# The seven-product steps of a feed-forward kernel made twice as wide: two weight slots per step, 512 columns per product

## The chip, the cores and the metric

The kernel runs on one core of one Trainium2 chip. The metric is the device time of one execution in microseconds (us).

## The reference

One macaron layer over 256 tokens of width 2048, all in float32: half a SwiGLU feed-forward, a mixer (gated short convolution beside a sparse attention), another half feed-forward, and a final RMSNorm.

```
def swiglu(h, wg, wu, wd):
    return (jax.nn.silu(h @ wg) * (h @ wu)) @ wd
...
        x = x + 0.5 * swiglu(rmsnorm(x, ffn1_norm[i]), ffn1_wg[i], ffn1_wu[i], ffn1_wd[i])
        x = x + hybrid_mixer(rmsnorm(x, mix_norm[i]), w_in[i], conv_w[i],
...
        x = x + 0.5 * swiglu(rmsnorm(x, ffn2_norm[i]), ffn2_wg[i], ffn2_wu[i], ffn2_wd[i])
    return rmsnorm(x, final_norm)
```

D_MODEL is 2048 and D_FF 5632. The change touches the two feed-forwards alone.

## The kernel before, in words

**Slots.** Every weight is read once, in slots of 256 rows by 512 columns (two k-tiles of 128 rows; 512 KB). There are four slot buffers (`SLOTS`), and slot c lives in buffer c % 4. SP loads it into `raw`. ACT rounds it to `w_hi` (`hi`, L1236), DVE takes the remainder `w_lo = raw - w_hi` (`lo`, L1726), and TensorE multiplies the 256 tokens (two tiles of 128) by it (`group`, L739 to L741). Each float32 product is made of three matmuls: hi by hi, hi by lo, lo by hi. So a plain slot is 2 k-tiles x 2 token tiles x 3 = 12 matmuls of 512 columns.

**What waits for what.** `hi` of slot c waits for its landing and until TensorE has finished slot c - 4 (`group_done`). `lo` waits for `hi`, and its semaphore `lo_ready` lets TensorE start the slot and lets SP load slot c + 4. Each engine works through its own list in program order: whatever DVE has listed ahead of the `lo` of a slot holds TensorE up if it ends late.

**Seven-product slots.** In 115 of the 528 feed-forward slots the 2 x 2 blocks (two token tiles, two k-tiles, two column halves of 256) are multiplied with seven products in place of eight (the Strassen-Winograd scheme): `seven_products`, L764 to L766, is 21 matmuls of 256 columns. DVE makes four sums of weight blocks (`weight_sums`, L1793, L1796, L1798; buffer `wt`, two of them), ACT and DVE split them (`wt_hi` L1291, `wt_lo` L1806). Some products go straight into the result's banks, the others collect in PSUM banks 6 and 7. After the last seven-product slot of a job ACT copies one bank (`products_copy`, L1300), DVE combines them in `z` (`products_sum`, L1837 to L1842) and adds the result to the bank (`add_to_bank`, L1852) or to `x` (`add_to_x`, L1861).

**Order.** Per feed-forward: 11 chunks of 512 hidden columns, each 8 gate slots (banks 0 and 1) and then 8 up slots (banks 2 and 3). Chunks 1 to 10 hold three seven-product slots each, at places 6, 12 and 14 (`SEVEN_AT`). After chunks 0 to 5 comes the first down part (`down(0)`), after chunks 6 to 10 the second (`down(1)`): four column chunks of the output, 12 and 10 slots each, of which four and three are seven-product slots (in one column chunk two). The finished column chunk is added to `x` by `residual` (L1919). In the last column chunk of the program the last four slots are run for token tile 0 first and then for tile 1 (`tail`). The order of the slots is a list written out by hand (`down_order`), and DVE's and ACT's other steps are hung behind the slot of a given number. POOL moves the SwiGLU output's blocks by DMA (`gu_blocks`, L681), and ACT and DVE split it for the down part (`gu_operand`, L1325, L1899).

## Time and profile before

| | |
|---|---|
| median of 3 runs | 1846.38 us (1846.32 to 1847.37) |
| the profiled execution, its own time | 1847.15 us |
| its span, first to last instruction | 1845.3 us |
| granted TensorE clock, mean | 0.999 |
| busy share PE / DVE / ACT / POOL | 99% / 80% / 55% / 13% |
| DMA | 60.2% of the 16 engines' span, 199 GB/s |

PE is TensorE's matmuls, PEld its weight loads (they overlap), DVE VectorE, ACT ScalarE, POOL GpSimd, SP the queue that issues the loads. Matmuls are pipelined: one is listed with 0.39 us and the next begins 0.23 us after it, so a stretch is costed by the distance from start to start. "Releaser" is what ended an engine's wait.

### The profile page before, as it was taken

Reading aid. Unit: us, or ns where it says so; the run is one execution under the profiler, and the core shown is the slowest. Engines: PE = TensorE matmul, PEld = TensorE weight load, DVE = VectorE, ACT = ScalarE, POOL = GpSimd, SP = SyncE. Lnnn points to the kernel's source line nnn. Section 1 sums busy time; section 2 is a strip of 40 time slices with the busy share of each in tenths; the row PEclk is TensorE's granted clock in tenths of the full one; section 3 lists DMA queues with packets and bytes.
Section 4 is the critical chain, followed back from the end, with each engine's and each line's share of the span. In section 5 each row is a group of like instructions: output and inputs, shape, how many; then the busy total and the mean of one; then the engine's idle time right before and its main releaser. Section 6 shows DMA issues by size and latency. Waiting matters only on the chain.

```text
span 1845.3 us, 26275 instructions
## 1 busy us (share of the span) xinstructions
PE 1835.3 (99%) x9415; PEld 1560.1 (85%) x9415; DVE 1477.2 (80%) x1971; ACT 1007.5 (55%) x1309; POOL 244.8 (13%) x442
## 2 busy tenths in 40 slices
PE   9999999999999999999999999999999999999998
PEld 7888888888888888888788888888888888888887
DVE  6788889877888887678677866688889887888897
ACT  7555555444555565556567746454555545555554
POOL 1111111001111100000132200111111000221100
PEclk9999999999999999999999999999999999999999
DMA  7666666566666666766443655666676666666664
GB/s 262 195 207 215 207 203 212 196 203 209 206 205 205 200 200 203 217 209 198 142 140 100 217 183 193 207 195 206 203 221 201 205 199 193 211 215 209 217 195 158
DMA packets 199280, 367.19 MB, mean 199 GB/s; under 512 B 19012, under 2 KB 23856, under 8 KB 199056
## 3 DMA queue, kind: packets, MB, share of 16 engines
q1 hardware_dynamic: 185008, 352.37, 60.2%
q0 software_dynamic: 11648, 12.02, 2.2%
q10 hardware_dynamic: 2528, 1.52, 0.3%
q8 instruction: 61, 1.00, 0.2%
q14 instruction: 35, 0.29, 0.1%
HBM read 350.11 MB, written 4.19 MB: 192 GB/s over the span
## 4 chain that ended last, share of the span: by engine, by line
PE 96%; DVE 1%; ACT 1%; DMA 0%; issue 0%; POOL 0%; ACTq 0%; POOLq 0%; DVEq 0%
PE ps L739 26%; PE ps L740 26%; PE ps L741 26%; PE ps L766 5%; PE ps L765 5%; PE ps L764 5%; PE ps L797 2%; DVE w_lo L1726 1%; POOL gu_raw L681 0%; PE ps L1003 0%; PE ps L1030 0%; PE ps L1005 0%; PE ps L1031 0%; DMA gu_raw<-gu_sq 0%; PE ps L1133 0%
## 5 line engine op out<-in xcount | busy, mean ns | idle before, releaser
L1726 DVE TENSOR_TENSOR w_lo<-raw,w_hi 128x1024 fp32r<-128x1024 f32 x540 | 656.6, 1227 | 190.0 <-ACT w_hi L1236 187.8
L1236 ACT ACTIVATE w_hi<-raw 128x1024 fp32r<-128x1024 f32 x540 | 566.3, 1057 | 341.2 <-PE ps L741 299.0
L739 PE MATMUL ps<-w_hi,hT_hi 128*128 128x512 f32 x1516 | 593.7, 392 | 0.1
L740 PE MATMUL ps<-w_lo,hT_hi 128*128 128x512 f32 x1516 | 590.9, 390 | 0.0
L741 PE MATMUL ps<-w_hi,hT_lo 128*128 128x512 f32 x1516 | 590.4, 389 | 0.0
L741 PEld LDWEIGHTS ps<-w_hi,hT_lo 128*128 128x128 f32 x1516 | 284.6, 188 | 60.5
L681 POOL DMA_DIRECT2D gu_raw<-gu_sq x352 | 187.1, 540 | 1110.5 <-DVE gu_sq L1910 1033.0
L739 PEld LDWEIGHTS ps<-w_hi,hT_hi 128*128 128x128 f32 x1516 | 285.0, 188 | 57.1 <-DVE w_lo L1726 0.8
L740 PEld LDWEIGHTS ps<-w_lo,hT_hi 128*128 128x128 f32 x1516 | 285.0, 188 | 55.3
L1291 ACT ACTIVATE wt_hi<-wt 128x1024 fp32r<-128x1024 f32 x115 | 122.0, 1061 | 154.5 <-DVE wt L1798 154.5
L739 PE MATMUL ps<-w_hi,guT_hi 128*128 128x512 f32 x484 | 189.5, 391 | 1.0 <-DVE w_lo L1726 0.7
L740 PE MATMUL ps<-w_lo,guT_hi 128*128 128x512 f32 x484 | 189.0, 391 | 0.0
L741 PE MATMUL ps<-w_hi,guT_lo 128*128 128x512 f32 x484 | 188.3, 389 | 0.0
L1806 DVE TENSOR_TENSOR wt_lo<-wt,wt_hi 128x1024 fp32r<-128x1024 f32 x115 | 140.7, 1223 | 21.5 <-ACT wt_hi L1291 21.5
L1289 ACT ACTIVATE w_hi<-raw 128x768 fp32r<-128x768 f32 x115 | 97.3, 846 | 109.9 <-PE ps L741 92.1
L1804 DVE TENSOR_TENSOR w_lo<-raw,w_hi 128x768 fp32r<-128x768 f32 x115 | 109.3, 951 | 1.5 <-ACT w_hi L1289 1.5
L739 PEld LDWEIGHTS ps<-w_hi,guT_hi 128*128 128x128 f32 x484 | 91.1, 188 | 19.4 <-DVE w_lo L1726 1.4
L741 PEld LDWEIGHTS ps<-w_hi,guT_lo 128*128 128x128 f32 x484 | 90.9, 188 | 19.4
L740 PEld LDWEIGHTS ps<-w_lo,guT_hi 128*128 128x128 f32 x484 | 91.1, 188 | 16.8
L1793 DVE TENSOR_TENSOR wt<-raw 128x512 f32<-128x512 f32 x115 | 78.5, 683 | 0.0
L1300 ACT ACTIVATE z<-ps 128x512 f32<-128x512 f32 x56 | 33.5, 598 | 76.1 <-PE ps L766 76.1
L703 POOL TENSOR_SCALAR prob<-prob,sums,gate 128x128 f32<-128x128 f32 (+1 forms) x64 | 37.1, 589 | 257.5 <-DVE sums L2169 257.5
(298 smaller groups left out, 2423.3 us busy)
## 6 DMA issues: line engine op xcount, KB each, us to landing
raw<-in_ffn_wu_dram SPq DMA_DIRECT2D x176, 512.0 KB, 4.4
raw<-in_ffn_wd_dram SPq DMA_DIRECT2D x176, 512.0 KB, 4.5
raw<-in_ffn_wg_dram SPq DMA_DIRECT2D x175, 512.0 KB, 3.6
raw<-in_w_in_dram SPq DMA_DIRECT2D x88, 512.0 KB, 3.6
raw<-in_w_out_dram SPq DMA_DIRECT2D x32, 512.0 KB, 4.7
gu_raw<-gu_sq POOLq DMA_DIRECT2D x352, 32.0 KB, 3.6
x_parked<-x SPq DMA_DIRECT2D x8, 256.0 KB, 5.1
raw<-in_cmp_k_w_dram SPq DMA_DIRECT2D x8, 256.0 KB, 2.9
```

What stands on the lines that cost most here:

```text
L681: pool.dma_start(gu_raw[c_ * SQ:c_ * SQ + SQ, :, a_, :], gu_sq[a_ * SQ:a_ * SQ + SQ, :, c_ * P:c_ * P + P]).then_inc(gu_moved, 16)
L739: mm(o, x_hi, w_hi[:, s, kk, :], start=first and kk == 0, stop=False)
L740: mm(o, x_hi, w_lo[:, s, kk, :], start=False, stop=False)
L741: ins = mm(o, x_lo, w_hi[:, s, kk, :], start=False, stop=last and kk == GK - 1)
L764: mm(o, x_hi, y_hi[:, blk], start=opens, stop=False, skip_group_check=True)
L765: mm(o, x_hi, y_lo[:, blk], start=False, stop=False, skip_group_check=True)
L1236: act.activation(w_hi[:, c % SLOTS, :, :], raw[:, c % SLOTS, :, :], ACT.Copy).then_inc(hi_ready, 1)
L1289: act.activation(flat(w_hi, s)[:, HC:], flat(raw, s)[:, HC:], ACT.Copy).then_inc(hi_ready, 1)
L1291: act.activation(wt_hi[:, b, :], wt[:, b, :], ACT.Copy).then_inc(t_hi_ready, 1)
L1726: tt(w_lo[:, s, :, :], raw[:, s, :, :], w_hi[:, s, :, :].bitcast(F32), ALU.subtract).then_inc(lo_ready, 1)
L1804: tt(flat(w_lo, s)[:, HC:], flat(raw, s)[:, HC:], flat(w_hi, s)[:, HC:].bitcast(F32), ALU.subtract)
L1806: tt(wt_lo[:, b, :], wt[:, b, :], wt_hi[:, b, :].bitcast(F32), ALU.subtract).then_inc(lo_ready, 1)
```

## The change

A seven-product step now covers two slots that follow one another: the same two k-tiles of the gate and of the up chunk (`PAIR`, `PAIR2`), or of two down column chunks. The two column halves of the 2 x 2 scheme are these two chunks, so every product has 512 columns: 21 matmuls of 512 columns for two slots. There are 68 such pairs in place of 115 single slots: two in each of the 20 chunks, and 4 and 3 in each of the two halves of a down part.

- **Order.** In a chunk the gate slots of k 0 to 4 come first, a pair, gate 5, up 0 and 1, a pair, up 2 to 5. A down part is two halves (`h`); each half works on two column chunks at once, left in banks 0 and 1, right in banks 2 and 3.
- **Banks.** The four collected products have a bank each, 4 to 7. A pair raises `group_done` by two at its end, and waits for `lo_ready` of its second slot after two of seven products.
- **Weight sums.** `wt` has one buffer of 4 x 512 columns. `weight_sums` needs both slots landed and the pair before finished on TensorE. The second slot's `w_hi` and `w_lo` are taken for one k-tile only.
- **Combining.** ACT copies the first product's bank (`product1_copy`). In a chunk DVE runs six operations of 512 columns behind place 14 (`gate_products`), and one of 1024 in the next chunk (`up_products`). In a down half it runs `left_residual`, nine operations in a row, behind place 24 of part 0 (for the second half: behind place 0 of the next chunk) and behind places 18 and 38 of part 1.
- In the transition to the mixer the transposes and operands of `x` come at other places (`x_transposes`, `x_operand`).

The core of the diff:

```diff
+GATE, UP, PAIR, PAIR2 = range(4)
+FIRST = [(GATE, j) for j in range(JD)] + [(UP, j) for j in range(JD)]
+CHUNK = [(GATE, 0), (GATE, 1), (GATE, 2), (GATE, 3), (GATE, 4), (PAIR, 6), (PAIR2, 6), (GATE, 5),
+         (UP, 0), (UP, 1), (PAIR, 7), (PAIR2, 7), (UP, 2), (UP, 3), (UP, 4), (UP, 5)]
+H_QUAD = {6: 0, 7: 1}
+PAIRS_AT = [p for p, (kind, _) in enumerate(CHUNK) if kind == PAIR]
+PAIRS = len(PAIRS_AT)
+
+
+LEFT, RIGHT = GATE, UP
+DOWN = [[(LEFT, 0), (LEFT, 2), (LEFT, 4), (LEFT, 6), (PAIR, 1), (PAIR2, 1), (LEFT, 8), (LEFT, 9),
+         (RIGHT, 0), (PAIR, 3), (PAIR2, 3), (RIGHT, 2), (RIGHT, 4), (RIGHT, 6), (PAIR, 5), (PAIR2, 5),
+         (LEFT, 10), (LEFT, 11), (RIGHT, 8), (RIGHT, 9), (PAIR, 7), (PAIR2, 7), (RIGHT, 10), (RIGHT, 11)],
+        [(LEFT, 0), (LEFT, 2), (LEFT, 4), (LEFT, 6), (PAIR, 1), (PAIR2, 1), (LEFT, 7), (RIGHT, 0),
+         (RIGHT, 2), (PAIR, 3), (PAIR2, 3), (RIGHT, 4), (LEFT, 8), (LEFT, 9), (PAIR, 5), (PAIR2, 5),
+         (RIGHT, 6), (RIGHT, 7), (RIGHT, 8), (RIGHT, 9)]]
...
+            def seven_products(f, c, hi, lo, k, s_hi, s_lo, job, first, last, i=None):
...
+                s = c % SLOTS
                 x = lambda kk, t: (hi[:, k + kk, t * P:t * P + P], lo[:, k + kk, t * P:t * P + P])
                 sm = lambda n: (s_hi[:, n - 1, :], s_lo[:, n - 1, :])
...
-                    ins = mm(o, x_lo, y_hi[:, blk], start=False, stop=closes, skip_group_check=True)
-                ins.then_inc(group_done, 1)
+                w = lambda u, kk: (w_hi[:, s + u, kk, :], w_lo[:, s + u, kk, :])
...
+                product(2, sm(4), w(1, 1), start=first)
+                product(PROD5, sm(1), d(T1), first, last)
+                product(PROD7, sm(3), d(T3), first, last)
+                product(PROD6, sm(2), d(T2), first, last)
+                product(1, x(1, 1), d(T4), stop=last).then_inc(group_done, 2)
 
             def compressed_group(c, j):
 
@@ -803,6 +790,8 @@
                     pe.wait_ge(x_landed[n], 16)
                 else:
                     pe.wait_ge(resid_done, resid(R_FFN1B if which == 1 else R_ATT, n))
+                    if which == 1 and n < 2:
+                        pe.wait_ge(prod_free, job_no(0, ("down", 1, n)) + 1)
                 for b in range(2):
                     if which == n == 0 and b == 0:
...
+            def slot(f, c, kind, i=None):
+
+                if kind == PAIR2:
+                    wt_high(f, c - 1, 1, i)
+                    hi_pair2(c, i)
+                else:
+                    hi(c, i, CHUNK_SLOTS)
+                    if kind == PAIR:
+                        wt_high(f, c, 0, i)
+
+            def product1_copy(f, key, done, i=None):
+
+
+                job = job_no(f, key)
+                act.wait_ge(group_done, count(done, i, CHUNK_SLOTS))
+                if job:
+                    act.wait_ge(prod_used, count(job, i, 1))
+                act.activation(z[:, 1, :], ps[:, PROD1, :], ACT.Copy).then_inc(prod1_copied, 1)
 
             def hs_high(f):
...
-                no = seven_no(f, c - FFN0[f])
-                b = SEVEN_SLOTS[f][SEVEN_NO[f, c - FFN0[f]]][0]
-                before = [c1 for b1, c1 in SEVEN_SLOTS[f][:SEVEN_NO[f, c - FFN0[f]]] if b1 == b]
-                dve.wait_ge(landed[s], landed_value(c, i, CHUNK_SLOTS))
+                s, no = c % SLOTS, pair_no(f, c)
+                for u in range(2):
+                    dve.wait_ge(landed[s + u], landed_value(c + u, i, CHUNK_SLOTS))
                 if i is not None:
-                    dve.wait_ge(group_done, count(c - JD + 1, i, CHUNK_SLOTS))
-                elif before:
-                    dve.wait_ge(group_done, FFN0[f] + before[-1] + 1)
-                w, o = flat(raw, s), wt[:, b, :]
-                two = lambda v: v.rearrange("p (a n) -> p a n", a=2)
-                tt(two(o[:, 0:CH]), w[:, 0:HC].unsqueeze(1).to_broadcast([P, 2, HC]), two(w[:, HC:HC + CH]),
+                    before = c - 3 if (c - FFN0[f]) % CHUNK_SLOTS == PAIRS_AT[1] else c - 9
+                    dve.wait_ge(group_done, count(before, i, CHUNK_SLOTS))
+                elif c != FFN0[f] + PAIR_SLOTS[0]:
+                    dve.wait_ge(group_done, FFN0[f] + PAIR_SLOTS[PAIR_SLOTS.index(c - FFN0[f]) - 1] + 2)
+                w = raw[:, s:s + 2, :, :].rearrange("p u k n -> p (u k) n")
+                tt(wt[:, T1:T3 + 1, :], w[:, 2, :].unsqueeze(1).to_broadcast([P, 2, CH]), w[:, 0::3, :],
                    ALU.subtract).then_inc(t1_ready, 1)
-                dve.wait_ge(t1_ready, count(no + 1, i, len(SEVEN_AT)))
-                tt(o[:, T2], w[:, B22], o[:, T1], ALU.subtract).then_inc(t2_ready, 1)
...
+            def wt_low(f, c, half, i=None):
+                dve.wait_ge(t_hi_ready, count(2 * pair_no(f, c) + half + 1, i, 2 * PAIRS))
+                sl = slice(2 * half, 2 * half + 2)
+                tt(wt_lo[:, sl, :], wt[:, sl, :], wt_hi[:, sl, :].bitcast(F32), ALU.subtract)
+
+            def slot(f, c, kind, next_kind, i=None):
+
+                if kind == PAIR2:
+                    s = c % SLOTS
+                    wt_low(f, c - 1, 1, i)
+                    dve.wait_ge(hi_ready, count(c + 1, i, CHUNK_SLOTS))
+                    tt(w_lo[:, s, 1, :], raw[:, s, 1, :], w_hi[:, s, 1, :].bitcast(F32),
+                       ALU.subtract).then_inc(lo_ready, 1)
+                else:
+                    lo(c, i, CHUNK_SLOTS)
+                    if kind == PAIR:
+                        wt_low(f, c, 0, i)
+                if next_kind == PAIR:
+                    weight_sums(f, c + 1, i)
 
             def h_sums(f):
 
 
-                pick = lambda buf: buf[:, 8:16, :].rearrange("p (q r) t -> p q r t", q=2)[:, :, 0:2, :]
-                h = z[:, :].rearrange("p (q r t) -> p q r t", q=2, r=2)
...
+            def product_sums(f, key, i=None):
+
+
+                no = count(job_no(f, key) + 1, i, 1)
+                tt(z[:, 1, :], ps[:, PROD6, :], z[:, 1, :], ALU.add).then_inc(prod_d, 1)
+                dve.wait_ge(prod_d, no)
+                tt(z[:, 0, :], ps[:, PROD5, :], z[:, 1, :], ALU.add).then_inc(prod_f, 1)
+                tt(z[:, 1, :], ps[:, PROD7, :], z[:, 1, :], ALU.add).then_inc(prod_e, 1)
+                dve.wait_ge(prod_e, no)
+
+            def last_sum(f, key, i=None):
+                dve.wait_ge(prod_f, count(job_no(f, key) + 1, i, 1))
+                tt(z[:, 1, :], ps[:, PROD7, :], z[:, 0, :], ALU.add).then_inc(prod_free, 1)
+
+            def gate_products(f, n, i=None):
+
+                dve.wait_ge(prod1_copied, count(job_no(f, n) + 1, i, 1))
+                tt(ps[:, 0, :], ps[:, 0, :], z[:, 1, :], ALU.add)
+                product_sums(f, n, i)
+                tt(ps[:, 1, :], ps[:, 1, :], z[:, 1, :], ALU.add).then_inc(gate_added, 1)
+                dve.wait_ge(gate_added, count((NFC - 1) * f + n, i, 1))
+                last_sum(f, n, i)
+
+            def up_products(f, n, i=None):
+
+                dve.wait_ge(group_done, count(FFN0[f] + chunk_slot(n) + CHUNK_SLOTS, i, CHUNK_SLOTS))
+                dve.wait_ge(prod_free, count(job_no(f, n) + 1, i, 1))
+                tt(ps[:, 2:4, :], ps[:, 2:4, :], z[:, :, :], ALU.add).then_inc(prod_used, 1)
+                dve.wait_ge(prod_used, count(job_no(f, n) + 1, i, 1))
+
+            def left_residual(f, part, h):
+
+                key = ("down", part, h)
+                job = job_no(f, key)
+                dve.wait_ge(group_done, FFN0[f] + down_slot(part, h) + left_end(part))
+                n, done = 2 * h, 2 * (2 * (2 * f + part) + h)
+                cols = slice(n * CH, n * CH + CH)
+
+                def add(t):
+                    stt(out=x[:, t, cols], in0=z[:, 1, :], scalar=0.5, in1=x[:, t, cols], op0=ALU.mult,
+                        op1=ALU.add).then_inc(left_added, 1)
+                    dve.wait_ge(left_added, done + t + 1)
+
+                for t in range(NT):
+                    stt(out=x[:, t, cols], in0=ps[:, t, :], scalar=0.5, in1=x[:, t, cols], op0=ALU.mult,
+                        op1=ALU.add).then_inc(left_read, 1)
+                dve.wait_ge(prod1_copied, job + 1)
+                dve.wait_ge(left_read, done + 2)
+                add(0)
+                product_sums(f, key)
+                add(1)
+                last_sum(f, key)
                 dve.wait_ge(prod_free, job + 1)
-                o = x[:, :, n * CH:n * CH + CH]
-                stt(out=o, in0=z_tiles, scalar=0.5, in1=o, op0=ALU.mult, op1=ALU.add).then_inc(prod_added, 1)
-                dve.wait_ge(prod_added, job + 1)
+                right = x[:, :, n * CH + CH:n * CH + 2 * CH]
+                stt(out=right, in0=z[:, :, :], scalar=0.5, in1=right, op0=ALU.mult, op1=ALU.add).then_inc(prod_used, 1)
+                dve.wait_ge(prod_used, job + 1)
+                dve.sem_inc(resid_done, NT)
...
+                    left_at = {left_end(part) + 2 + h * width: h for h in range(NDC // 2)}
+                    for g, (h, p, kind, _) in enumerate(order):
+                        slot(f, c + g, kind, order[g + 1][2] if g + 1 < len(order) else None)
                         if g == 2:
-                            add_to_bank(f, n_last, 1)
+                            up_products(f, n_last)
                             up(f, n_last)
                         if g == 3:
                             gu_transpose(f, n_last)
-                        if g == (11 if part == 0 else 10):
+                        if g == (12 if part == 0 else 10):
                             gu_operand(f, n_last, None)
-                        if c + g in sums_at:
-                            products_sum(f, "down", part, sums_at[c + g])
-                            add_to_x(f, part, sums_at[c + g])
-                        if c + g in resid_at:
-                            n = resid_at[c + g]
-                            residual(n, FFN0[f] + down_end(f, part, n), n % 2, half)
+                        if g in left_at:
+                            left_residual(f, part, left_at[g])
+                        if g == width + 2:
+                            residual(1, FFN0[f] + down_slot(part, 1), 1, half)
                         if part == 1:
-                            if f == 0 and g in (20, 28, 38):
-                                x_operand(1, (20, 28, 38).index(g))
-                            if f == 1 and g in (17, 25, 35):
```

How the lists of the engines changed, at two places.

The first place is DVE in the first feed-forward, first down part, from the end of one output piece into the next (names are `w_lo`, `z`, `x` as above, `ps` is PSUM). Before, the end of the first column chunk: splits of three slots, `products_sum`, `add_to_x`, two splits, weight sums, `residual`.

```order
L1726 TENSOR_TENSOR w_lo<-raw,w_hi 128x1024 [waits hi_ready] x3
L1837 TENSOR_TENSOR z<-z 128x256 [waits prod_copied]
L1839 TENSOR_TENSOR z<-ps,z 128x256 [waits prod_d]
L1840 TENSOR_TENSOR z<-ps,z 128x256
L1842 TENSOR_TENSOR z<-ps,z 128x256 [waits prod_f]
L1861 SCALAR_TENSOR_TENSOR x<-z,x 128x2x512 [waits prod_free]
L1726 TENSOR_TENSOR w_lo<-raw,w_hi 128x1024 [waits hi_ready,prod_added]
```

These were five operations between two splits. Now, at the end of the first half, stand the splits of slots 22, 23 and 24, then `left_residual`, then the splits of slots 25 and 26.

```order
L1736 TENSOR_TENSOR w_lo<-raw,w_hi 128x1024 [waits hi_ready] x3
L1893 SCALAR_TENSOR_TENSOR x<-ps,x 128x512 [waits group_done]
L1893 SCALAR_TENSOR_TENSOR x<-ps,x 128x512
L1888 SCALAR_TENSOR_TENSOR x<-z,x 128x512 [waits left_read,prod1_copied]
L1853 TENSOR_TENSOR z<-ps,z 128x512 [waits left_added]
L1855 TENSOR_TENSOR z<-ps,z 128x512 [waits prod_d]
L1856 TENSOR_TENSOR z<-ps,z 128x512
L1888 SCALAR_TENSOR_TENSOR x<-z,x 128x512 [waits prod_e]
L1861 TENSOR_TENSOR z<-ps,z 128x512 [waits prod_f,left_added]
L1903 SCALAR_TENSOR_TENSOR x<-z,x 128x2x512 [waits prod_free]
L1736 TENSOR_TENSOR w_lo<-raw,w_hi 128x1024 [waits prod_used,hi_ready]
L1736 TENSOR_TENSOR w_lo<-raw,w_hi 128x1024 [waits hi_ready]
```

Between the third split and the next one stood five operations, four of them of 256 columns; now there are nine of 512 columns or more.

The second place is DVE in a chunk, from the split of place 9 to the end of the second pair (places 10 and 11), now:

```order
L1736 TENSOR_TENSOR w_lo<-raw,w_hi 128x1024 [waits hi_ready] x3
L1801 TENSOR_TENSOR wt<-raw 128x1024 [waits group_done,landed3,landed2]
L1804 TENSOR_TENSOR wt<-raw,wt 128x512 [waits t1_ready]
L1806 TENSOR_TENSOR wt<-raw,wt 128x512 [waits t2_ready]
L1736 TENSOR_TENSOR w_lo<-raw,w_hi 128x1024 [waits hi_ready]
L1811 TENSOR_TENSOR wt_lo<-wt,wt_hi 128x1024 [waits t_hi_ready] x2
L1819 TENSOR_TENSOR w_lo<-raw,w_hi 128x512 [waits hi_ready]
```

Before, a seven-product slot had the same shape with one slot's columns (L1793, L1796, L1798, L1804, L1806) and a second `wt` buffer.

## Rows read from the trace of the kernel before

**Rows 1.** The page, busy time (share of the span) and instructions of each engine:

```profile
PE 1835.3 (99%) x9415; PEld 1560.1 (85%) x9415; DVE 1477.2 (80%) x1971; ACT 1007.5 (55%) x1309; POOL 244.8 (13%) x442
```

**Rows 2.** The waits, TensorE's own, whole span: total us, times, longest.

```profile
PE ps L852 <- DVE junk L2406: 1.2, 1, 1.2
PE ps L739 <- DVE w_lo L1726: 0.7, 1, 0.7
PE ps L818 <- DMA vec_rows<-in_ffn_norm_dram: 0.7, 1, 0.7
PE ps L739 <- DVE guT_lo L1899: 0.2, 1, 0.2
```

**Rows 3.** Timeline of PE over one chunk: start us, us, engine, line.

```profile
115.43 0.28 PE L764 MATMUL ps<-w_hi,hT_hi 128*128 128x256 f32 x1
...
142.09 0.39 PE L739 MATMUL ps<-w_hi,hT_hi 128*128 128x512 f32 x1
...
158.41 0.28 PE L764 MATMUL ps<-w_hi,hT_hi 128*128 128x256 f32 x1
...
160.92 0.40 PE L739 MATMUL ps<-w_hi,hT_hi 128*128 128x512 f32 x1
```

**Rows 4.** Timeline of DVE, feed-forward 1: starts and durations by size.

```profile
150.11 0.68 DVE L1793 TENSOR_TENSOR wt<-raw 128x512 f32<-128x512 f32 x1
150.83 0.43 DVE L1796 TENSOR_TENSOR wt<-raw,wt 128x256 f32<-128x256 f32 x1
...
305.20 1.28 DVE L1919 SCALAR_TENSOR_TENSOR x<-ps,x 128x512 f32<-128x512 f32 x2
...
397.14 2.36 DVE L1726 TENSOR_TENSOR w_lo<-raw,w_hi 128x1024 fp32r<-128x1024 f32 x2
```

**Rows 5.** Groups of DVE and ACT by form, 46 to 780 us: busy, mean ns.

```profile
L1726 DVE TENSOR_TENSOR w_lo<-raw,w_hi 128x1024 fp32r<-128x1024 f32 x213 | 257.2, 1218 | 83.6 <-ACT w_hi L1236 83.1
L1852 DVE TENSOR_TENSOR ps<-ps,z 128x1024 f32<-128x1024 f32 x20 | 24.5, 1224 | 0.0
L1919 DVE SCALAR_TENSOR_TENSOR x<-ps,x 128x512 f32<-128x512 f32 x16 | 10.2, 682 | 0.8 <-PE ps L741 0.8
L1861 DVE SCALAR_TENSOR_TENSOR x<-z,x 128x1024 f32<-128x1024 f32 x8 | 9.8, 1226 | 0.3
...
L1236 ACT ACTIVATE w_hi<-raw 128x1024 fp32r<-128x1024 f32 x213 | 223.7, 1057 | 149.0 <-PE ps L741 136.0 <-PE ps L766 7.8 <-DMA raw<-in_ffn_wd_dram 4.6
```

**Rows 6.** Timeline, all engines, at a slot's end (TensorE's next slot begins, ACT follows).

```profile
144.81 0.39 PE L739 MATMUL ps<-w_hi,hT_hi 128*128 128x512 f32 x1
...
145.01 1.06 ACT L1236 ACTIVATE w_hi<-raw 128x1024 fp32r<-128x1024 f32 x1 [1.65 <-PE ps L741]
```

**Rows 7.** Busy time of each engine in a chunk's length, PEclk, DMA share, GB/s.

```profile
138.00:181.00 43.00, 43.00 (x221) 36.86 (x220) 36.22 (x48) 22.69 (x26) 8.50 (x16) 1.00 0.66 207
```

**Rows 8.** Timeline near the end: the last four slots.

```profile
1829.88 1.22 DVE L1726 TENSOR_TENSOR w_lo<-raw,w_hi 128x1024 fp32r<-128x1024 f32 x1
1830.09 0.39 PE L741 MATMUL ps<-w_hi,guT_lo 128*128 128x512 f32 x1
...
1831.15 0.50 PE L739 MATMUL ps<-w_hi,guT_hi 128*128 128x512 f32 x1 [0.68 <-DVE w_lo L1726]
...
1831.49 0.40 PE L740 MATMUL ps<-w_lo,guT_hi 128*128 128x512 f32 x1
```

**Rows 9.** Instructions on the tile `raw`, 297 to 400 us: its loads.

```profile
DMA to landing us min/median/max: 3.4/4.2/5.4
```

**Rows 10.** Timeline of PE at the very start and the very end.

```profile
1.20 3.17 PE L852 MATMUL ps<-junk 128*128 128x512 bf16 x7 [1.20 <-DVE junk L2406]
...
6.97 2.50 PE L852 MATMUL ps<-junk 128*128 128x512 bf16 x6
...
9.86 0.39 PE L837 MATMUL ps<-w_lo,hT_hi 128*128 128x512 f32 x1
10.09 0.40 PE L838 MATMUL ps<-w_hi,hT_lo 128*128 128x512 f32 x1
...
1837.90 0.39 PE L741 MATMUL ps<-w_hi,guT_lo 128*128 128x512 f32 x1
```

**Rows 11.** Stretches at the end: us, PE busy, granted clock, DMA share, GB/s.

```profile
1841.00:1842.00 1.00, 0.00 (x0) 1.00 0.25 96
1842.00:1843.00 1.00, 0.00 (x0) 0.51 1.01 381
```

More of the change, by code:

```diff
@@ L355, in build_program @@
     at[0] = wt_at
-    wt = sb("wt", [P, 2, 4 * HC])
+    wt = sb("wt", [P, 4, CH])
     at[0] = gs_at
@@ L725, in _, with group @@
             mm = nc.tensor.matmul
-            def group(c, i, per, hi, lo, k, banks, first, last, tiles=range(NT), signal=group_done):
+            def group(c, i, per, hi, lo, k, banks, first, last, tiles=range(NT), signal=group_done, opened=(), skip=False):
                 pe.wait_ge(lo_ready, count(c + 1, i, per))
@@ L738, in group @@
                         x_lo = lo[:, k + kk, t * P:t * P + P]
-                        mm(o, x_hi, w_hi[:, s, kk, :], start=first and kk == 0, stop=False)
-                        mm(o, x_hi, w_lo[:, s, kk, :], start=False, stop=False)
-                        ins = mm(o, x_lo, w_hi[:, s, kk, :], start=False, stop=last and kk == GK - 1)
+                        begin = first and kk == 0 and t not in opened
+                        mm(o, x_hi, w_hi[:, s, kk, :], start=begin, stop=False, skip_group_check=skip)
```

394 lines of the change are left out of this document (164 added, 230 removed).

## The prediction

> **What bounds the kernel now.** I read the engines' busy shares first, then TensorE's own waits, then its timeline. PE is busy 99% of the span, DVE 80% [rows 1]; over the whole span PE waited for other engines under 3 us [rows 2]. So the time is the sum of TensorE's distances from start to start, and the timeline gives them. Between 142.09 and 158.41 stand 72 matmuls of 512 columns: 0.2267 us each, 2.72 us for a plain slot of 12. Between 158.41 and 160.92 stand the 21 matmuls of 256 columns of one seven-product slot: 2.51 us, 0.1195 each [rows 3]. The same place of the chunk before is at 115.43, so a chunk takes 42.98 us; less 13 plain slots (35.36) that leaves 2.54 for each of three seven-product slots: the matmuls just behind one come slightly late. In a chunk's 43 us DVE is busy 36.2 [rows 7]: it is the engine with the least room, and its list is in strict order.
>
> **TensorE's own saving.** Half the columns cost 0.1195 and not 0.1134, so a matmul has some 12 ns that don't shrink with its width; 21 of 256 columns pay them in full. A seven-product slot saves only 2.72 - 2.54 = 0.18 us today, 115 of them 20.7 us. A pair will be 21 x 0.2267 = 4.76 us against 5.44 for two plain slots: 0.68 saved, 68 pairs 46.2 us. Net **-25.5 us**. The transposes of `x` only move. The trace has no row of a pair, but it has these matmuls' shape 6000 times, so I put no more than 1 us of doubt on it.
>
> The Trainium skill ("TensorE: Matmul & The Clock Gate", section "Back-to-back issue gap") gives N / 2.4 + 2.5 ns, 216 and 109 ns for the two widths. That speaks against this change: single slots would already save 0.30 us, and the net would be 44.1 - 34.2 = 10 us, as an estimate by that page. The rows disagree by 10 ns at both widths.
>
> **What DVE pays for it.** DVE's operations begin 1.14 us apart at 1024 columns (2.36 for two less 1.22) and 0.60 at 512 (1.28 less 0.68); where the next one needs the result, 0.72 at 512 (150.11 to 150.83) and 1.22 + 0.04 = 1.26 at 1024 [rows 4, 5]. Reading PSUM makes no difference: 682 and 1224 ns [rows 5]. ACT starts 0.20 us after TensorE's next slot begins and takes 1.06 for a split [rows 5, 6]. A split that ends late costs its end + 0.16: it ended at 1831.10, and the second matmul came at 1831.49, so the first was worth 1831.26 [rows 8].
>
> **The chunk fits, narrowly.** Let a pair end at 0. Then 3 slots follow and the next pair, whose second half is due at 3 x 2.72 + 6 x 0.2267 = 9.52. A pair reports both of its slots only at its end, so the split of the third slot can't begin earlier: ACT 0.20 to 1.26, DVE from 1.30. Then DVE's spacing is 1.14 (split), 1.26 + 0.72 + 0.60 (weight sums), 1.14 (split), 2 x 1.14 (`wt_lo`), and 0.68 for the half split: end 9.12, with 0.16 it is 9.28. Room: **0.24 us**. There are 36 such places: one in each of 20 chunks, two in each of 8 down halves. I cost them at nothing; what hides them is exactly these three slots. Behind place 14 the six operations of `gate_products` take 0.60 + 0.72 + 0.60 + 3 x 0.72 = 4.08; from the end of the second pair DVE reaches its split of place 14 at 1.30, ends these at 6.5 and the split of place 15 at 7.7, due at 8.16. This fits by 0.3. The whole list of a chunk comes to some 37.5 us of 42.2. Landings: a load takes 3.4 to 5.4 us [rows 9], and the weight sums come some 6 us behind the split that frees the buffer in a chunk, 5 us in a down part; below 1 us in all.
>
> **`left_residual` does not fit.** It stands behind the split of a slot that itself had to wait for the pair's end. DVE is free at 1.30 + 1.14 = 2.44. The nine operations take 0.60 + 0.72 (two from PSUM to `x`) + 0.72 (`add`) + 0.72 + 0.60 + 0.72 (sums) + 0.72 (`add`) + 0.72 + 1.26 = 6.78, so the next split runs from 9.22 to 10.44 and counts from 10.60. TensorE has three plain slots, 8.16 us. It stalls **2.4 us**. Before, four operations of 256 and one of 1024 columns stood there: 1.5 + 1.3 us, which hid. Of the eight places seven are of this kind: 17.1 us. The eighth is place 38 of the last down part, where the last four slots are run for tile 0 first: slot 39 is due after 3 x 1.36 = 4.08, so the stall is 6.5, less the 0.9 that stands at the same place today (1830.32 to 1831.26) [rows 8]: 5.6 us.
>
> Late next: SP can load slot 29 of part 0 only after the split of slot 25 (10.44); with 4.2 us to land the weight sums start at 14.7 and the second half of that pair counts from 14.7 + 6.68 + 0.16 = 21.5, due at 10.6 + 9.52 = 20.1: 1.4 us, twice, 2.8 (0.6 each at the shortest landing). At the start of a down part the first pair comes one place earlier than in a chunk, behind `up` and its sums: some 0.15 us, four times, 0.6. In the mixer's first slots `x_operand` for three column chunks comes late, but DVE stays 2 us or more ahead: nothing.
>
> The clock: the granted clock was 1.00 until 1842 and then 0.51, its lower level (1.2 GHz), 3.7 us after the last matmul's end at 1838.3 [rows 10, 11]. The stall of 6.5 us is longer than that, so the last 30 matmuls can begin at the lower level. The first seven matmuls of the program came 0.45 apart, the next six 0.42, and from 9.86 on 0.23 [rows 10]. Bounds: nothing, or 30 x 0.22 = 6.6. I take 2.5, eleven matmuls, since the slow group at the start, six long, is the nearest. The same page of the Trainium skill (section "Part 1: The HAM clock gate") says that an idle array falls back to 1.2 GHz and must be busy again to regain 2.4; the trace's end agrees, and by it some of this cost is certain.
>
> **Sum.** -25.5 + 17.1 + 5.6 + 2.8 + 0.6 + 2.5 = +3.1 us. The profiled execution took 1847.15 (span 1845.3), so 1850.3; the median of the runs is 0.77 below it, so I forecast **1849.5 us**. Two large terms cancel. A measurement of this kernel can tell about 0.2%, 3.7 us, from no change, so this is just inside "no change", on its slower edge.
>
> **The rivals.**
> 1. *The 36 narrow places don't hold* (slower). For: 0.24 us is less than the spread of one landing, and a chunk's DVE list is at 89%. Against: each spacing in that chain has its row. From 0.24 us too long on, every excess counts 36-fold: at 0.5 us of error it is 9 us, 1859.
> 2. *`left_residual` hides* (faster). For: DVE is idle about 7 us in 43 [rows 7], and if its list got ahead by 2.4 us the stall would vanish. Then 5.6 at the tail becomes about 3, the clock stays, and it is -25.5 + 4 = 1825; with half of the stalls 1835. Against: the split in front of it waits for the pair's end, so DVE cannot get ahead there.
> 3. *The width is worth less than the rows say*, the change not doing what it is meant to. If the fixed part of a matmul were none, 0.1072 us per 256 columns, a single slot would have saved 0.32 and a pair 0.64: net 7 us, 1868. Against: the 2.51 is measured. This is the direction of the page's rule above.
>
> **How the numbers follow.** The forecast's mechanism 0.62, with a range of its own from 1843 (no clock loss, stalls of 2.1) to 1855 (all 30 matmuls slow, stalls of 2.7): of this 0.04 faster, 0.30 within 0.2%, 0.28 slower. Rival 1: 0.25, slower. Rival 2: 0.10, faster. Rival 3: 0.03, slower. Together faster 0.14, same 0.30, slower 0.56. The range of 8 in 10 leaves out most of rival 2 and the far end of rivals 1 and 3: 1840 to 1862.
>
> **What would show it.** Right: the distance from start to start stays 0.227 in pairs, a chunk takes 42.2 us, PE's waits name `w_lo` with seven stalls near 2.4 us and one near 6.5 close to the end, nothing at the chunks' pairs, and DVE runs L1893 to L1903 in 6.8 us. Wrong: waits of a few tenths for the half split L1819 in every chunk (rival 1), no stall behind L1903 (rival 2), or 0.24 and more between the matmuls of a pair (rival 3).

## The result and the profile after

The change made the kernel slower: 1876.3 us median (1874.4 to 1878.52, 4 runs) against 1846.55 on the same chip, ratio 1.0161, 95% interval 1.0143 to 1.0178. The forecast was 1849.5, its range ended at 1862. The profiled execution took 1874.4, its span is 1872.6.

The page, busy time and instructions of each engine, and the chain that ended last (in [rows 1] PE was busy 99% with 9415 matmuls):

```profile
PE 1824.8 (97%) x8176; PEld 1493.7 (80%) x8176; DVE 1486.6 (79%) x1767; ACT 1000.3 (53%) x1302; POOL 245.8 (13%) x442
...
PE 81%; DVE 12%; DMA 5%; ACT 1%; issue 1%; ACTq 0%; DVEq 0%
```

DVE and DMA together hold 17% of the chain. TensorE's own waits of the changed kernel (total us, times, longest); before, none for `w_lo` was above 0.7 [rows 2]:

```profile
PE ps L722 <- DVE w_lo L1736: 23.6, 8, 6.5
PE ps L740 <- DVE w_lo L1819: 14.0, 16, 1.2
...
PE ps L740 <- DVE w_lo L1736: 0.9, 2, 0.7
```

L722 is a plain slot's first matmul and L1736 its split; L740 opens each product of a pair, and L1819 is the half split on which the pair's second part waits. Both kinds of wait stand in the down parts, and the first kind also in the first slots of the chunk behind a first down part, where `left_residual` of its second half runs. No pair of a chunk waits, and the chunks are shorter than before. Busy time in one chunk's length (us, PE, PEld, DVE, ACT, POOL, then PEclk, DMA share, GB/s; answers to [rows 7]) and one pair in it, 125.43 to 130.19:

```profile
138.00:180.16 42.16, 42.16 (x188) 34.91 (x187) 37.32 (x43) 22.70 (x26) 8.53 (x16) 1.00 0.70 211
```

```profile
125.43 0.39 PE L740 MATMUL ps<-w_hi,hT_hi 128*128 128x512 f32 x1
...
126.79 0.39 PE L740 MATMUL ps<-w_hi,hs_hi 128*128 128x512 f32 x1
...
127.92 0.39 PE L742 MATMUL ps<-wt_hi,hs_lo 128*128 128x512 f32 x1
```

Dividing the program where the steady chunks begin and end (from the timelines, first matmul of a stage to first matmul of the next, the last stage up to the last matmul) gives the whole picture. The stall that `left_residual` makes in the first slots of chunk 6 (2.8 us; 4.3 with the slower matmuls behind it in feed-forward 2) is counted with the down part before it. The last two columns are experiments that follow below.

| stage, us | before | change | up weights read | wide chunks only |
|---|---|---|---|---|
| start to chunk 1 | 56.1 | +0.6 | +0.3 | +0.4 |
| four stages of steady chunks, 20 chunks | 859.6 | -16.4 | -16.3 | -16.4 |
| first down part, feed-forward 1 | 127.9 | +9.7 | +5.7 | -0.1 |
| second down part, mixer, chunk 0 | 558.0 | +11.8 | +7.7 | -0.2 |
| first down part, feed-forward 2 | 128.1 | +9.3 | +6.5 | +0.6 |
| second down part to the end | 108.1 | +12.2 | +11.2 | +0.7 |

So the chunks gave all that was asked of them, and the four stages with the down parts lost some 43 us where 28 wide pairs should have saved 9. From the last matmul's start to the end of the program it is 7.5 us in both kernels.

### The profile page after: what moved, and what is told of

It reads as the page before. It is cut to its first block, busy times and chain, and to the rows that moved or that the text cites. A ratio compares the mean times of both kernels' runs of the same rounds, so it can differ in the third digit from the quotient of the medians.

```text
span 1872.6 us, 23493 instructions
## 1 busy us (share of the span) xinstructions
PE 1824.8 (97%) x8176; PEld 1493.7 (80%) x8176; DVE 1486.6 (79%) x1767; ACT 1000.3 (53%) x1302; POOL 245.8 (13%) x442
## 4 chain that ended last, share of the span: by engine, by line
PE 81%; DVE 12%; DMA 5%; ACT 1%; issue 1%; ACTq 0%; DVEq 0%
PE ps L722 21%; PE ps L724 21%; PE ps L723 21%; PE ps L740 5%; PE ps L742 5%; PE ps L741 5%; DMA raw<-in_ffn_wd_dram 5%; DVE w_lo L1736 4%; DVE wt_lo L1811 2%; PE ps L784 2%; DVE wt L1801 1%; ACT w_hi L1236 1%; DVE wt L1804 1%; DVE wt L1806 1%; DVE w_lo L1819 1%
## 5 line engine op out<-in xcount | busy, mean ns | idle before, releaser
L1736 DVE TENSOR_TENSOR w_lo<-raw,w_hi 128x1024 fp32r<-128x1024 f32 x587 | 711.1, 1227 | 247.8 <-ACT w_hi L1236 245.2
L1236 ACT ACTIVATE w_hi<-raw 128x1024 fp32r<-128x1024 f32 x587 | 608.6, 1056 | 474.9 <-PE ps L742 222.5
L722 PE MATMUL ps<-w_hi,hT_hi 128*128 128x512 f32 x1436 | 563.0, 392 | 4.9 <-DVE w_lo L1736 4.9
L724 PE MATMUL ps<-w_hi,hT_lo 128*128 128x512 f32 x1436 | 560.1, 390 | 0.0
L723 PE MATMUL ps<-w_lo,hT_hi 128*128 128x512 f32 x1436 | 559.7, 390 | 0.0
L722 PEld LDWEIGHTS ps<-w_hi,hT_hi 128*128 128x128 f32 x1436 | 270.1, 188 | 60.6 <-DVE w_lo L1736 6.4
L1287 ACT ACTIVATE wt_hi<-wt 128x1024 fp32r<-128x1024 f32 x136 | 144.4, 1062 | 148.0 <-DVE wt L1801 121.8
L722 PE MATMUL ps<-w_hi,guT_hi 128*128 128x512 f32 x480 | 189.9, 396 | 18.7 <-DVE w_lo L1736 18.7
L1811 DVE TENSOR_TENSOR wt_lo<-wt,wt_hi 128x1024 fp32r<-128x1024 f32 x136 | 160.1, 1218 | 0.0
L722 PEld LDWEIGHTS ps<-w_hi,guT_hi 128*128 128x128 f32 x480 | 91.4, 190 | 40.3 <-DVE w_lo L1736 21.4
L1801 DVE TENSOR_TENSOR wt<-raw 128x1024 f32<-128x1024 f32 x68 | 83.0, 1221 | 27.5 <-DMA raw<-in_ffn_wd_dram 14.0
L1330 ACT ACTIVATE gu<-ps,rs 128x512 f32<-128x512 f32 x44 | 27.9, 686 | 63.8 <-DVE ps L1868 63.3
L1804 DVE TENSOR_TENSOR wt<-raw,wt 128x512 f32<-128x512 f32 x68 | 47.1, 692 | 2.3
L1806 DVE TENSOR_TENSOR wt<-raw,wt 128x512 f32<-128x512 f32 x68 | 47.0, 692 | 2.3
```

Source lines behind the costliest of these rows:

```text
L722: mm(o, x_hi, w_hi[:, s, kk, :], start=begin, stop=False, skip_group_check=skip)
L723: mm(o, x_hi, w_lo[:, s, kk, :], start=False, stop=False, skip_group_check=skip)
L724: ins = mm(o, x_lo, w_hi[:, s, kk, :], start=False, stop=last and kk == GK - 1, skip_group_check=skip)
L1236: act.activation(w_hi[:, c % SLOTS, :, :], raw[:, c % SLOTS, :, :], ACT.Copy).then_inc(hi_ready, 1)
L1287: act.activation(wt_hi[:, 2 * half:2 * half + 2, :], wt[:, 2 * half:2 * half + 2, :], ACT.Copy).then_inc(t_hi_ready, 1)
L1736: tt(w_lo[:, s, :, :], raw[:, s, :, :], w_hi[:, s, :, :].bitcast(F32), ALU.subtract).then_inc(lo_ready, 1)
```

## Theory and rival

Theory after reading: two separate mechanisms. (A) `left_residual` stands in front of a split that TensorE needs (predicted), and the long idle times it makes also drop the clock. (B) In the down parts the second slot of a pair lands too late, so the weight sums and with them the half split come late (not predicted). Rival: DVE's list in a down part is simply too long, and either cure only moves the wait.

The rows behind B: two neighbouring pairs of the same shape, on DVE. First a chunk, where the sums begin at 119.71 and the pair at 125.43, 5.72 us later:

```profile
119.71 1.22 DVE L1801 TENSOR_TENSOR wt<-raw 128x1024 f32<-128x1024 f32 x1
120.96 0.69 DVE L1804 TENSOR_TENSOR wt<-raw,wt 128x512 f32<-128x512 f32 x1
...
125.70 0.68 DVE L1819 TENSOR_TENSOR w_lo<-raw,w_hi 128x512 fp32r<-128x512 f32 x1
```

Then the second pair of the first down part, which begins at 293.31, only 3.86 us behind its sums. DVE stood idle 2.07 us for the landing:

```profile
289.45 1.23 DVE L1801 TENSOR_TENSOR wt<-raw 128x1024 f32<-128x1024 f32 x1 [2.07 <-DMA raw<-in_ffn_wd_dram]
...
295.45 0.68 DVE L1819 TENSOR_TENSOR w_lo<-raw,w_hi 128x512 fp32r<-128x512 f32 x1
```

The three loads in question were issued 1.13 us apart at 281.24, 282.37 and 283.50. Instructions on the tile `raw` in that stretch, and then in a chunk (121 to 127 us, two loads 2.9 apart):

```profile
L558 SPq DMA_DIRECT2D raw<-in_ffn_wd_dram x3: 367/367/368, 281.2 to 283.5; - x3
DMA to landing us min/median/max: 4.4/7.0/7.4
```

```profile
L558 SPq DMA_DIRECT2D raw<-in_ffn_wu_dram x2: 373/373/373, 123.5 to 126.4; - x2
DMA to landing us min/median/max: 3.7/3.7/3.7
```

Why three leave together: ACT had rounded the two slots behind the pair by 279.76, but their splits stand in DVE's list behind the pair's sums, `wt_lo` and half split. The half split and these two then run back to back, and each one's end (281.21, 282.35, 283.48) lets SP issue a load. The split after them waits for the pair's end:

```profile
277.54 2.22 ACT L1236 ACTIVATE w_hi<-raw 128x1024 fp32r<-128x1024 f32 x2
...
280.53 0.68 DVE L1819 TENSOR_TENSOR w_lo<-raw,w_hi 128x512 fp32r<-128x512 f32 x1
281.13 2.35 DVE L1736 TENSOR_TENSOR w_lo<-raw,w_hi 128x1024 fp32r<-128x1024 f32 x2
286.15 1.23 DVE L1736 TENSOR_TENSOR w_lo<-raw,w_hi 128x1024 fp32r<-128x1024 f32 x1 [2.67 <-ACT w_hi L1236]
```

The chunks have such groups too. The loads for the chunk pair above were issued at 113.56 and 115.06, with a third at 112.56, and landed sooner (`raw`, 112 to 116 us):

```profile
DMA to landing us min/median/max: 4.1/4.4/4.6
```

So three loads in a group are not enough to make a pair late. All 20.3 us by which the down pairs took too long (the "excess" below) stand at pairs whose sums began within 0.15 us of the second slot's landing.

## The experiments

Each ratio is against the kernel before on the same chip. Its medians there lie between 1846.6 and 1848.4 us, so a difference between the medians of two experiments is uncertain by 1 to 2 us, and the change's own four runs spread over 4. "Excess" below is, in the profiled execution, the sum over the 28 down pairs of (time from the pair's first matmul to the first behind it, less 4.76 us). It is 20.3 us in the change, and 0.0 over its 40 chunk pairs.

### left_residual one place later

```
-                    left_at = {left_end(part) + 2 + h * width: h for h in range(NDC // 2)}
+                    left_at = {left_end(part) + 3 + h * width: h for h in range(NDC // 2)}
```

and in chunk 6 at place 1 instead of 0.

> The nine operations of left_residual are hung one slot later, everything else as in the change. Theory A (the stalls of 2.6 us come from these operations standing between the pair's end and the next split): DVE is free at 1.30 + 2 x 1.14 = 3.58 us after the pair's end, ends them at 10.4, and the next split counts from 11.7 against 10.9 due, so seven stalls of 2.6 us become 0.9, the one of 6.5 us near the end goes, and with it the stretches at half clock (some 5.6 us): 1876 - 12 - 6 - 6 = 1852 us. Rival (that split waits for a landing or for ACT at that place, and left_residual only happens to stand there): the stalls stay near 2.6 and the time within 3 us of 1876.

1861.1 us, ratio 1.0074 (1.0057 to 1.009): 15 us less than the change, not the 24 expected. TensorE's waits:

```profile
PE ps L740 <- DVE w_lo L1819: 18.7, 22, 1.2
PE ps L722 <- DVE w_lo L1736: 6.5, 7, 1.3
```

The wait for plain slots fell from 23.6 to 6.5, mechanism A, and the granted clock stayed at 1.00 until the last matmul had ended. The wait inside pairs grew from 14.0 to 18.7 (excess 25.4, and 1.8 more in chunk 6): what A gave back, the pairs took in part. The end of the program took another part, as the next experiment shows.

### left_residual in two pieces

The first six operations stay, the last three (`add(1)`, `last_sum`, the right half) follow one or two slots later; the tail's stand behind the last split.

```
+                    pieces = [(left_at[0], 0, 0), (left_at[0] + (1 if f == 0 and part == 1 else 2), 0, 1)]
+                    if part == 1 and f == 0:
+                        pieces += [(left_at[1], 1, 0), (left_at[1] + 1, 1, 1)]
+                    if part == 1 and f == 1:
+                        pieces += [(left_at[1] + 1, 1, 0), (left_at[1] + 1, 1, 1)]
```

> left_residual cut in two: the first six operations at the old place, the last three one or two slots later; in the last half of the program all of it behind the last split; one residual moved a slot later. Theory A: no split is late at that place any more, seven stalls of 2.6 us, the one of 6.5 us and some 5.6 us of half clock go, while about 1 us comes back at each first pair of a following half, where DVE has less time: 1848 us. The stalls at the pairs of the down parts (14 us in the profile) stay. Rival (the clock loss comes from something else than these stalls): the granted clock still shows stretches at 0.5 inside the program and the time is 5 us longer than that.

1859.05 us, ratio 1.0066 (1.0049 to 1.0082); missed by 11 in the same direction:

```profile
PE ps L740 <- DVE w_lo L1819: 17.9, 23, 1.2
PE ps L722 <- DVE w_lo L1736: 2.9, 3, 2.0
```

Mechanism A is all but gone (2.9 us of its wait are left), the kernel is 17 us faster, and the granted clock stays at 1.00 until the last matmul has ended. What is missing from the expectation stands in two places. The pairs' excess rose to 23.8 us, with 3.2 more in chunk 6: 6.7 us together. And from the last matmul's start to the end it now takes 12.4 us in place of 7.5, because the tail's `left_residual` stands between the last split and the final norm: 4.9 us. The same 4.9 us are in each experiment that puts it there (one place later, both cures, the tail alone, the pieces with other weights).

### The load behind a pair held back

In the down parts SP's load that comes right behind a pair waits for one more split.

```
-                    sp.wait_ge(lo_ready, count(c - SLOTS + 1, i, per))
+                    sp.wait_ge(lo_ready, count(c - SLOTS + 1 + held, i, per))
...
+                             held=int(g >= SLOTS and down_job(part)[g - 1][2] == PAIR2))
```

> In the down parts SP issues the load of the slot just behind a pair one split later; DVE, ACT and TensorE as in the change. Theory B (the pairs of the down parts stall because the second slot's load, issued 1.1 us before the next one, shares the DMA engines with it and lands after 6 to 7 us, so the weight sums of both slots come late): the stalls on the half split at the pairs fall from 14 us to about 6, and the time from 1876 to 1868. Rival (the load is late because its buffer is freed late, and sharing costs nothing): landings and stalls stay, 1876 us; if holding the load makes the slot behind the pair late, it is above 1880.

1867.7 us, ratio 1.0111 (1.0094 to 1.0128), as expected. Lines stand one lower:

```profile
PE ps L723 <- DVE w_lo L1737: 23.6, 8, 6.5
...
PE ps L741 <- DVE w_lo L1820: 7.1, 10, 1.2
```

A load was issued later and the kernel became 8.6 us faster. That speaks for B and against a DVE list that is too long: no operation of DVE was touched. The excess fell from 20.3 to 11.6, by 8.7. The second slot's load of the pair above took 6.2 us in place of 7.0 (`raw`, 278.7 to 281.1 us, the first and the second slot's load), and the median of these landings over the 28 down pairs went from 5.7 to 5.1 us:

```profile
DMA to landing us min/median/max: 5.3/5.7/6.2
```

### Both cures together

> Both edits together: left_residual in two pieces, and the load behind a pair in the down parts held for one more split. Theory (the 29.8 us are two separate mechanisms, left_residual's stalls with the half clock they bring, and the late second slot of a pair in the down parts): the second takes off here about what it took off alone, 8.6 us of 1876.3, so 1850 to 1852 us, and the wait of the pair's bank 2 matmul on the half split L1819 falls from 17.9 us to 7 to 10. Rival (the two share their cause: a chain of splits that is late for either reason, and whichever is removed the other takes its place): 1857 to 1860 us, nothing gained over the pieces alone.

1852.66 us (1851.73 to 1853.48), ratio 1.0025 (1.0015 to 1.0035). Against the pieces alone it took off 6.4 us (7.6 by the two ratios), and excess 17.2 stands beside 23.8. Alone the two edits took off 17.3 and 8.6, together 23.6, so the two mechanisms are separate in the main and the rival at 1857 to 1860 us falls. It is right in part: with `left_residual` moved or cut the pairs wait longer than without. The wait for L1820, 14.3 us, did not come down to the 7 to 10 that I had put. That the second piece of `left_residual` now stands nearer to the next pair may be why; it wasn't tried. Of the 4.3 us by which this kernel is still behind the one before, the 4.9 to 5.0 behind the last matmul are more than all. The old tail with these two cures was not tried either.

### The tail alone

```
+                        if f == part == 1 and g == len(order) - 1:
+                            left_residual(f, part, 1)
```

> The change with one edit: the last left_residual of the program, which stood before the last slot's split, stands behind it. It prices the tail alone. Theory (TensorE waits 6.5 us there for the split, and 8 matmuls after it run at 0.43 instead of 0.2267 us): 6.5 + 1.6 come back less 1 to 3 us by which x's last columns come later at the end, so 1869 to 1872 us. Rival (the 6.5 us only move: the nine operations then stand before the last residual and the end of the program is as late as it was): 1875 to 1877 us.

1871.49 us (1871.37 to 1874.31), ratio 1.013, in the expected range; the 6.5 us wait is out of the row:

```profile
PE ps L722 <- DVE w_lo L1736: 17.1, 7, 2.4
PE ps L740 <- DVE w_lo L1819: 13.3, 17, 1.2
```

The stage from the second down part to the last matmul went from +12.2 to +5.6, but behind the last matmul it takes 12.5 us in place of 7.5. Of 6.6 us gained, 4.9 are paid again, where I had put 1 to 3. The medians differ by 4.8 us and the profiled executions by only 2.9, so that the time fell into the expected range is in part luck.

### Where the loads read from

Three runs leave out the product with the down weights: the loads of the down parts, same in number, size, queue and order, read other weights.

```
-                        load(c + g, wd[f][:, k:k + GK, n * CH:n * CH + CH])
+                        load(c + g, wu[f][:, k % KD:k % KD + GK, n * CH:n * CH + CH])
```

> The change, but the loads of the down parts read blocks of the up projection's weights (rows 22.5 KB apart) in place of the down projection's (rows 8 KB apart): same number, size, queue and order of loads; the product with the down weights is left out. It asks whether the late second slot comes from where the data lies or from three loads issued within 2.3 us of each other. If from where it lies: the loads of the down parts land as those of the chunks do (3.6/4.4/5.5 us), the wait of the pair's bank 2 matmul on L1819 falls from 14.0 us to under 6, time 1864 to 1868 us. If from the burst: landings of 7 us stay behind each pair, the wait stays at 12 to 15 us, time 1873 to 1878 us.

1861.67 us, ratio 1.0078 (1.0061 to 1.0094): 14.6 us less than the change (12.1 between the profiled executions), by another address alone. TensorE's waits:

```profile
PE ps L722 <- DVE w_lo L1736: 23.6, 8, 6.5
...
PE ps L740 <- DVE w_lo L1819: 3.5, 8, 0.8
```

and the pair that began 3.86 us behind its sums, now with the wait for the landing down from 2.07 to 0.52:

```profile
286.54 1.23 DVE L1801 TENSOR_TENSOR wt<-raw 128x1024 f32<-128x1024 f32 x1 [0.52 <-DMA raw<-in_ffn_wu_dram]
```

Row A (23.6) is untouched to the tenth, row B all but gone, excess 7.2.

> left_residual in two pieces (1859.05 us alone, wait on L1819 17.9 us) with the same replaced reads in the down parts; the product with the down weights is left out. Where the data lies decides: the wait falls below 9 us and the time to 1848 to 1852 us. The burst decides: 1857 to 1861 us with the wait at 16 to 19 us.

1848.52 us (1846.22 to 1850.76), ratio 1.0009 (0.9999 to 1.0019), wait on L1819 8.6 us: 10.5 off the pieces alone.

The control reads `w_out`, whose rows lie as far apart as the down weights' and whose blocks are as few as those read from the up weights:

> Control for the two runs that read the up weights: the loads of the down parts read blocks of the output projection's weights, whose rows lie 8 KB apart as the down weights' do, and which is as small and as often read again as the blocks of the up weights were (16 row blocks in place of 44); the product with the down weights is left out. If the spacing of the rows makes the landings late: as the change itself, 1873 to 1878 us with a wait on L1819 of 12 to 16 us. If it was the smaller, repeated area: as the run with the up weights, 1860 to 1864 us with a wait of 3 to 5 us.

1868.47 us (1867.4 to 1871.81), ratio 1.0113, between the two expectations. Its profiled span is 1870.0, 2.6 below the change's, and the wait stays near the change's (excess 17.4):

```profile
PE ps L740 <- DVE w_lo L1819: 11.7, 15, 1.2
```

The three loads at the same place landed in 4.4/7.0/7.4 us from the down weights, 4.3/6.0/6.7 from `w_out`, 4.2/5.5/6.1 from the up weights. Over all groups of three in the down parts (issued within 2.7 us, none in the 1.6 us before) the second load took 5.9 us in the median from the down weights, 5.7 from `w_out` and 4.9 from the up weights. So most of the difference in waiting (8.2 of the 10.5 us) goes with rows 8 KB apart against 22.5 KB. The time says less: 6.8 of 14.6 us by the medians, 9.6 of 12.1 by the profiled executions. The rest goes with the smaller area or its placing, which these runs don't separate. And the crowding has its own share: with the up weights too a load in a group of three took 6.1, where two loads 2.9 apart took 3.7.

### Wide in the chunks, single in the down parts

If all of the loss is in the down parts, then the change's chunks with the down parts, hand-overs and tail of before must beat both. The pair code keeps its semaphores, the single steps get their own, and they meet at two places:

```
+                if first:
+                    if n == 0:
+                        pe.wait_ge(prod_free, pair_jobs_done(f, part))
+                    else:
+                        pe.wait_ge(one_free, one_no(f, "down", part, n))
...
+                                pe.wait_ge(one_free, one_no(f, "down", 0, NDC - 1) + 1)
```

> Pairs of slots with 512 columns in the ten steady chunks only; the down parts, the chunk-to-down and down-to-mixer transitions and the tail as in the kernel before (seven products on one slot, 256 columns, banks 6 and 7, x sums by products_sum and add_to_x). Theory (all of the loss sits in the down parts and the tail; the chunks keep their 4.1 us per four chunks, 20 chunk executions at 0.82 us each): 1846.5 - 16.4 = 1830 us, down parts within 1 us each of the kernel before, no half-clock stretch inside the program. Rival 1 (the saving in the chunks is paid again where the pair's banks hand over to the single steps, at chunk 6 and at each down part's first seven-product step): 1834 to 1840 us. Rival 2 (the memory side or the clock gives way at the higher rate of the chunks): over 1842 us.

1832.04 us median (1830.99 to 1832.79, 4 runs) against 1848.4, ratio **0.9911** (0.9895 to 0.9928): 16.4 us faster than before. That it is the chunks' share to the tenth is chance: the interval reaches from 13 to 19 us, and the profiled spans differ by 14.9, the chunks' 16.4 less 1.4 at the other stages. Page and chain:

```profile
PE 1819.3 (99%) x8754; PEld 1521.7 (83%) x8755; DVE 1497.9 (82%) x1871; ACT 1005.5 (55%) x1309; POOL 244.9 (13%) x442
...
PE 96%; DVE 1%; DMA 1%; ACT 0%; POOL 0%; issue 0%; ACTq 0%; POOLq 0%; DVEq 0%
```

DVE's share is higher here than in either kernel and TensorE waits for it some 2 us in all (1.3 us on the half split, 0.8 on an operand). So DVE's load as such is not the bound; what stands in its list at a given place can be.

## Why the prediction was wrong, step by step

| term of the sum, us | predicted | seen |
|---|---|---|
| TensorE's own saving | -25.5 | -16.4 in the chunks, measured; -9.1 in the down parts by the same pair length |
| the 36 narrow places | 0 | 0.0 at the 20 in the chunks, +12.8 at the 16 in the down parts |
| `left_residual`, seven places | +17.1 | +18.2 (2.6 each) |
| `left_residual` at the tail | +5.6 | +6.0 |
| the other 12 pairs of the down parts (1.4 twice, 0.6; landings anywhere "below 1 us in all") | +3.4 | +7.5 |
| clock | +2.5 | +5.7 |
| sum | +3.1 | +24.7 of 27.25; the other 2.5 in gaps of a few tenths, 1.6 of it in the matmul behind each of the eight stalls (0.34 or 0.59 us) |

**TensorE's own saving** was right: 0.2267 us per matmul in a pair, 4.76 us a pair, a chunk 42.16 where I wrote 42.2. Rival 3 would have made 20 chunks save some 6 us in place of 16.4. The rule of the Trainium skill ("TensorE: Matmul & The Clock Gate", section "Back-to-back issue gap") behind it would have given some 8 us, an estimate by that page's figures; it puts a matmul of 512 columns at 0.216 us where the trace has 0.2267.

**The chunk fits, narrowly** was right for the chunks and wrong for the down parts. The 0.24 us of room was claimed for 36 places; at the 20 in the chunks nothing was late, at the 16 in the down halves 12.8 us were lost, at up to 1.7 us a place. So rival 1 occurred in part, and by the first reason that it gave for itself, the spread of one landing. Its sign, waits in every chunk, did not come, and its count of 36 equal losses did not either.

**`left_residual` does not fit** was right in mechanism, place and size. DVE in front of the tail's split, 1848.21 to 1855.20, is 6.99 us where the sum had 6.78:

```profile
1848.21 1.28 DVE L1893 SCALAR_TENSOR_TENSOR x<-ps,x 128x512 f32<-128x512 f32 x2
...
1853.82 1.22 DVE L1903 SCALAR_TENSOR_TENSOR x<-z,x 128x1024 f32<-128x1024 f32 x1
1855.20 1.23 DVE L1736 TENSOR_TENSOR w_lo<-raw,w_hi 128x1024 fp32r<-128x1024 f32 x1 [0.15 <-DVE x L1903]
```

**The step that failed is the one on landings**, 17 of the 24 us that were missing (20.3 where 3.4 were put). It said "a load takes 3.4 to 5.4 us [rows 9]" and "below 1 us in all". What the runs showed is 20.3 us, all at pairs whose sums began at the landing of their second slot. The weight sums of a pair need both of its slots, so the later landing counts. The pair at 293.31 shows it: its second slot's load was issued at 282.37 and took 7.0 us, 1.6 beyond the longest that I allowed. The sums began at 289.45, and the chunk's spacing would have had them at 287.6. Further on it is the same: three loads from 350.3 on took 3.9, 6.0 and 6.2, and the sums at 357.50 waited for the second (issued at 351.4). That landings are the cause is shown by the runs that changed nothing else: another address left 7.2 us of the 20.3, the load behind each pair held back 11.6.

Rows 9 were also too narrow a sample. Their stretch began at 297 us, just behind two loads of the kernel before that took 5.9 and 6.0 (`raw`, 265 to 297 us):

```profile
DMA to landing us min/median/max: 3.7/4.9/6.0
```

The longest landing of a down-part load in that whole trace is 7.9 us (issued at 1739.04).

In those down parts loads left in a group of three six times and then took 4.0, 5.9 and 6.1 us (medians). In the change it is 25 times, with 4.0, 5.9 and 6.1; with the load held back it is 8 times. A group is not slower than it was; there are more of them, and a pair's second slot is now often the second load of one. I had carried the chain from split to load to landing to sums through once, behind `left_residual` ("late next"), with the median landing; it had to be carried through behind every pair, with the landing of loads in a group. That one term, 1.4 us twice, came out at 1.6 and 0.0: at the second place the load landed in 3.6 us in place of 4.4, and TensorE was late itself by slower matmuls.

The four first pairs of the down parts cost 5.5 us where I had 0.6. At the one of 278.44 the half split ended at 281.21 and the matmul behind it came at 281.26, where it was due at 279.80. Its sums too began at a landing (273.34), of a load issued at 267.18 as the second of a group that took 5.9, 6.1 and 6.3 us. And two transposes (L1953) stand between its sums and its half split, so that these are 7.9 us apart and not 6.7.

**The clock** was mis-sized. I had let only the stall of 6.5 us cost clock, because it is longer than the 3.7 us that passed at the program's end before the clock fell. But beside the tail, three of the seven other `left_residual` stalls, of 2.44 us each, were followed by matmuls at the lower level. TensorE after such a wait, and stretches there and at the tail, where the last three numbers are granted clock, DMA share and GB/s:

```profile
673.10 0.79 PE L722 MATMUL ps<-w_hi,guT_hi 128*128 128x512 f32 x1 [2.44 <-DVE w_lo L1736]
673.69 0.63 PE L723 MATMUL ps<-w_lo,guT_hi 128*128 128x512 f32 x1
674.12 0.63 PE L724 MATMUL ps<-w_hi,guT_lo 128*128 128x512 f32 x1
...
676.20 0.39 PE L723 MATMUL ps<-w_lo,guT_hi 128*128 128x512 f32 x1
```

```profile
674.00:677.00 3.00, 3.00 (x10) 2.33 (x10) 2.54 (x3) 1.42 (x2) 0.00 (x0) 0.65 0.85 251
1857.00:1860.00 3.00, 3.00 (x8) 2.30 (x7) 1.42 (x5) 1.20 (x2) 0.00 (x0) 0.50 0.00 0
```

Some 28 matmuls at 0.43 in place of 0.2267 are 5.7 us, eight of them at the tail. I had reckoned eleven, at the tail only.

**The chances.** 0.56 for slower was right in direction, but it reached to some 1855 (the forecast's own mechanism) and 1859 (rival 1). The sum itself stood just inside no change; what made the kernel clearly slower is the step above, which the sum had at next to nothing, so the direction is in part luck. The range added rivals to the sum one at a time; an error of 17 us in one step was outside all of them.

## What to carry to other kernels

When a step keeps an engine busy while other buffers become ready, the splits that waited behind it run back to back, and the loads that they release go out in a group. Price the landing of the load that the next step needs from loads in such groups, not from the median of spread ones, and do it at every place where the step recurs. Take the sample of landings from the whole stage: here a stretch that began at 297 us left out two of 5.9 and 6.0, issued in the 2 us before. A table by stage, made before any cure is tried, shows which part of a change to keep: here wide steps in the chunks, where no pair waited, and the old ones elsewhere gave 16.4 us, while curing the wide down parts took two edits and still ended 0.25% above the kernel before. Look at the end of the program by itself: work moved out of TensorE's way there cost 4.9 us behind the last matmul. Holding a load back can make a kernel faster (8.6 us here).

## What the runs showed of the hardware

- Loads of 512 KB whose rows of 2 KB lie 8 KB apart landed in 4.4, 7.0 and 7.4 us when three were issued within 2.3 us; from an array with rows 22.5 KB apart in 4.2, 5.5 and 6.1, at the same place. Over all such groups in the down parts the second load took 5.9 us against 4.9 (medians), and 5.7 from another array with rows 8 KB apart. Two loads 2.9 us apart (22.5 KB rows) took 3.7.
- The granted clock fell to its lower level (1.2 GHz) after some waits of 2.44 us: three of seven here, and four, four, four and five of seven in the runs with the load held, the tail alone, the up weights and `w_out`. The same place of the program had it in one run and not in another. It fell after none of 2.0 us or less in the runs with the pieces, with one place later, with both cures, and with wide chunks alone. What decides between the waits of 2.44 was not tried and stays open.
